# A product-key expert layer: 128 tokens' experts gathered row by row, 416 tokens through the dense product, u before v

## The reference, cut to what matters

```python
qh = (xt @ w_pq).reshape(PEER_BLOCK, PEER_HEADS, 2, half)
sub = einsum('thcd,ckd->thck', qh, sub_keys)
top_s, top_i = lax.top_k(sub, PEER_TOPK)
cand = (top_s[:, :, 0, :, None] + top_s[:, :, 1, None, :]).reshape(PEER_BLOCK, PEER_HEADS, 256)
best_s, best_c = lax.top_k(cand, PEER_TOPK)
...
experts = i1 * PEER_KEYS + i2
gate = jax.nn.softmax(best_s, axis=-1)
act = jax.nn.gelu(einsum('td,thkd->thk', xt, expert_u[experts]))
return einsum('thk,thkd->td', gate * act, expert_v[experts])
```

## Time and profile before

| | |
|---|---|
| median of three runs | 2608.47 us (2607.95 to 2617.67) |
| profiled execution | 2607.49 us |
| its span, first to last instruction | 2605.7 us |
| PE busy | 2344.5 us (90%), 12881 matmuls |
| DVE busy | 1535.3 us (59%) |
| POOL busy | 1064.4 us (41%) |
| ACT busy | 830.9 us (32%) |
| DMA | 411.09 MB |
| routing with 46 u blocks | about 914 to 1209 us |
| gate tables with 16 u blocks | about 1209 to 1507 us |
| value stage | about 1541 to 2594 us |

### The profile page before, as it was taken

The page is one execution under the profiler, slowest core; times in us unless marked ns, Lnnn a source line. Parts: engine busy times, 40 slices in busy tenths (PEclk is TensorE's granted clock), DMA queues, the critical chain, the costliest instruction groups (busy, mean ns, idle before and its releaser), DMA issues.

```text
span 2605.7 us, 36939 instructions
## 1 busy us (share of the span) xinstructions
PE 2344.5 (90%) x12881; PEld 1949.2 (75%) x12881; DVE 1535.3 (59%) x2958; ACT 830.9 (32%) x1293; POOL 1064.4 (41%) x568
## 2 busy tenths in 40 slices
PE   6999997775698999997777789999999999999998
PEld 5989557754488977776666668888888888888886
DVE  2567344333312089999999945555555555555555
ACT  3232332312223255553333332222222222222221
POOL 2334002310022244445777754444444445444442
PEclk9998579868998999998999999999999999999999
DMA  6441455428631143342433465555555555555553
GB/s 222 143 157 66 153 200 214 182 76 303 216 111 62 48 129 116 127 133 85 166 142 136 177 228 173 174 175 176 177 177 175 172 173 172 173 175 176 173 174 103
DMA packets 165036, 411.09 MB, mean 158 GB/s; under 512 B 11936, under 2 KB 82848, under 8 KB 159168
## 3 DMA queue, kind: packets, MB, share of 16 engines
q1 hardware_dynamic: 152672, 275.77, 32.6%
q10 hardware_dynamic: 3056, 100.53, 9.9%
q0 software_dynamic: 9216, 33.56, 3.4%
HBM read 351.95 MB, written 124.29 MB: 183 GB/s over the span
## 4 chain that ended last, share of the span: by engine, by line
PE 65%; issue 15%; POOL 10%; DVE 4%; DMA 3%; ACT 2%; SPq 1%; POOLq 0%; ACTq 0%; DVEq 0%; PEldq 0%
PE bank L2122 18%; PE bank L2124 18%; PE bank L2123 18%; POOL one L1497 6%; POOL u_lo L1591 3%; PE bank L427 1%; DMA ks<-kc 1%; PE bank L446 1%; PE bank L628 1%; SPq L937 1%; PE bank L618 1%; PE bank L627 1%; PE bank L436 1%; PE bank L2204 1%; PE bank L2195 1%
## 5 line engine op out<-in xcount | busy, mean ns | idle before, releaser
L1591 POOL TENSOR_TENSOR u_lo<-u_raw,u_hi 128x1024 fp32r<-128x1024 f32 x128 | 330.1, 2580 | 706.8 <-ACT u_hi L1573 706.8
L1716 DVE TENSOR_TENSOR y_t<-y_t,bank 128x512 f32<-128x512 f32 x512 | 351.9, 687 | 361.5 <-PE bank L2124 361.5
L2122 PE MATMUL bank<-hn_hi,u_hi 128*128 128x512 f32 x1024 | 409.0, 399 | 14.4 <-POOL u_lo L1591 13.7
L2124 PE MATMUL bank<-hn_hi,u_lo 128*128 128x512 f32 x1024 | 406.6, 397 | 0.0
L2122 PE MATMUL bank<-a_hi,v_hi 128*128 128x512 f32 x1024 | 400.1, 391 | 5.1 <-DVE a_lo L1711 5.1
L2123 PE MATMUL bank<-hn_lo,u_hi 128*128 128x512 f32 x1024 | 403.3, 394 | 0.0
L2123 PE MATMUL bank<-a_lo,v_hi 128*128 128x512 f32 x1024 | 399.6, 390 | 0.0
L2124 PE MATMUL bank<-a_hi,v_lo 128*128 128x512 f32 x1024 | 399.4, 390 | 0.0
L1772 POOL TENSOR_TENSOR v_lo<-v_raw,v_hi 128x1024 fp32r<-128x1024 f32 x128 | 304.8, 2405 | 8.7 <-ACT v_hi L1673 8.6
L2122 PEld LDWEIGHTS bank<-hn_hi,u_hi 128*128 128x128 f32 x1024 | 193.4, 189 | 65.0 <-POOL u_lo L1591 23.6
L2122 PEld LDWEIGHTS bank<-a_hi,v_hi 128*128 128x128 f32 x1024 | 192.6, 188 | 46.9 <-DVE a_lo L1711 5.2
(11 more groups left out here) (370 smaller groups left out, 4154.2 us busy)
## 6 DMA issues: line engine op xcount, KB each, us to landing
u_raw<-eu SPq DMA_DIRECT2D x128, 512.0 KB, 5.9
v_raw<-ev SPq DMA_DIRECT2D x128, 512.0 KB, 3.7
gates_dram<-gst ACTq DMA_DIRECT2D x8, 4096.0 KB, 12.2
gin<-gates_dram SPq DMA_DIRECT2D x64, 512.0 KB, 4.4
k_s<-kc ACTq DMA_DIRECT2D x29, 1104.0 KB
v_s<-vc ACTq DMA_DIRECT2D x29, 1104.0 KB
acts_dram<-act_c SPq DMA_DIRECT2D x64, 256.0 KB, 2.1
act_l<-acts_dram SPq DMA_DIRECT2D x64, 256.0 KB, 4.5
```

What stands on the lines that cost most here:

```text
L1591: nc.gpsimd.tensor_tensor(out=u_lo[s][:], in0=u_raw[s][:], in1=u_hi[s][:].bitcast(F32), op=ALU.subtract).then_inc(dn["ulo"], 1)
L1716: tt(out=y_t[:, x, :], in0=y_t[:, x, :], in1=bank[4 + x % 4][:], op=ALU.add).then_inc(dn["acc"], 1)
L2122: nc.tensor.matmul(out, ah, bh, start=first and i == 0, stop=False)
L2124: last = nc.tensor.matmul(out, al, bh, start=False, stop=final and i == n - 1)
```

## The change

128 of the 544 tokens (the last 96 of the prompt and the 32 sample tokens, `NG`) get their experts by index: they are routed first, each of their 128 picks is one indirect DMA that fetches one row of 1024 values for each of the 128 tokens, 128 fetches of u rows and then 128 of v rows, into three slots (`rows_g`). The other `DT` = 416 tokens go through the dense product. All 128 u blocks come first, in pairs with WINDOW = 6, 7, 7, 7, 6 beside the five routed tiles, two pairs beside each of eight gate blocks of 52 tokens, and 15 pairs behind them; then all 128 v blocks, with y accumulated in PSUM: its eight chunks stand in eight banks over all experts, and `accumulate` goes. All activations go through `acts_dram`, read for two experts at a time; gates are read for four.

The 128 dots stand on DVE between the steps of the routing (13 per tile from the second on), between the gate groups (46), and behind them (30). Of the 128 additions of v rows (`weigh`), 16 come before expert 2, the others at 112 of the places of experts 2 to 121. The fetches stand on POOL at matching places: those of u and the first 16 of v ahead of `lo_u` in each half of a pair, the others behind `lo_v` of an expert. One-hots are now made per token by tensor_scalar (compare with the pick, and in the second also multiply by the gate), and POOL's multiply goes. The core of the diff:

```diff
-GT = 64
-GBLOCKS = SEQ // GT
-SLOTS = P // (NB * NL)
-PICKS_S = PH * TOPK // SLOTS
+NG = 128
+DT = TOK - NG
+GBLOCKS = 8
+GT = DT // GBLOCKS
+PICKS = PH * TOPK
+ROUTE = [(DT, NG)] + [(t0, min(P, DT - t0)) for t0 in range(0, DT, P)]
+ROW_SLOTS = 3
...
-                        tt(out=one2[n % HOT][:], in0=bc(asc, 1, 4), in1=bc(cols_s[:, b % 2, 1, 4 * k:4 * k + 4], 2, PK), op=ALU.is_equal)
-                        tt(out=one1[n % HOT][:], in0=bc(asc, 1, 4), in1=bc(cols_s[:, b % 2, 0, 4 * k:4 * k + 4], 2, PK), op=ALU.is_equal)\
-                            .then_inc(ff["ones_raw"], 1)
+            for n in range(GBLOCKS * QUADS):
+                dve.wait_ge(ff["gate_mm"], n + 1)
+                for j in range(4):
+                    c = 4 * n + j
+                    ts(one2[n % HOT][:, j, :], asc, picks_t[:, 1, c:c + 1], None, ALU.is_equal)
+                    last = ts(one1[n % HOT][:, j, :], asc, picks_t[:, 0, c:c + 1], picks_t[:, 2, c:c + 1], ALU.is_equal, ALU.mult)
+                last.then_inc(ff["ones"], 1)
+                if n % QUADS % 2 and n >= HOT:
+                    dots(dve, NT, 1)
+            dots(dve, NT + 1, PICKS)
...
+            for x in range(XS):
                 for s in range(2):
-                    lo_u(pool, x + s, 1 - s)
-            pool_dense(pool, chain)
+                    for m in FETCH_X[2 * x + s]:
+                        fetch(pool, m)
+                    if s == 0 or x + 1 < XS:
+                        lo_u(pool, x + s, 1 - s)
+                if x in (FIRST_V, FIRST_V + 1):
+                    lo_v(pool, x - FIRST_V)
+            pool_dense(pool)
...
+        def fetch(pool, m):
+
+            if m == 0:
+                few_wait(pool, "idx", 1)
+            if ROW_SLOTS <= m < PICKS + ROW_SLOTS:
+                few_wait(pool, "dot", m - ROW_SLOTS + 1)
+            elif m >= PICKS + ROW_SLOTS:
+                few_wait(pool, "sum", m - ROW_SLOTS - PICKS + 1)
...
+        def dots(dve, stage, count):
+
+            for _ in range(min(count, DOTS[stage] - asked[stage])):
...
+                dve.wait_ge(row_in[n % ROW_SLOTS], 16 * (n // ROW_SLOTS) + 16)
+                row = rows_g[n % ROW_SLOTS][0:NG, :]
+                nc.vector.tensor_tensor_reduce(out=row, in0=row, in1=xrep[0:NG, :], scale=1.0, scalar=0.0, op0=ALU.mult, op1=ALU.add,
+                                               accum_out=pre_g[0:NG, n:n + 1]).then_inc(sx["dot"], 1)
...
+            def feed(i, q, last=False):
+
+                e = i * ROUND + q
+                if not last or q + 2 < ROUND:
+                    sp.wait_ge(dn["vlo"], e + 1)
+                    load_v(sp, e + 2, q % 2)
+                if q % 2 and (not last or q < 4):
+                    sp.wait_ge(dn["alo"], e + 1)
+                    load_acts(sp, i * (ROUND // 2) + (q // 2 + 2), q // 2 % 2)
+                if q % 4 == 3 and not last:
+                    sp.wait_ge(dn["mul"], e + 1)
+                    load_gates(sp, i * 2 + (q // 4 + 2), q // 4 % 2)
...
+            def outs(e, q, first=False, final=False):
+
+                pe.wait_ge(dn["alo"], e + 1)
+                pe.wait_ge(dn["vlo"], e + 1)
...
+        def act_value(act, f, q, arrived):
+
+            act.wait_ge(v_in[q % 2], arrived)
+            nc.scalar.activation(v_hi[q % 4][:], v_raw[q % 2][:], ACT.Copy).then_inc(dn["vhi"], 1)
+            act.wait_ge(dn["mul"], f + 1)
+            nc.scalar.activation(a_hi[q % 4][:], act_l[q // 2 % 2][:, q % 2, :], ACT.Copy).then_inc(dn["ahi"], 1)
...
+                f = i * ROUND + (q + 2)
+                act.wait_ge(dn["outs"], f + 1)
+                act_value(act, f, q + 2, i * (8 * ROUND) + (16 * ((q + 2) // 2) + 16))
...
+            for f in range(2, PK):
+                weight(f)
+                for m in FETCH_V[f - 2] if f - 2 < len(FETCH_V) else ():
+                    weigh(m - PICKS)
+                low(f)
...
+        def pool_dense(pool):
+            for f in range(2, PK):
+                lo_v(pool, f)
+                for m in FETCH_V[f - 2] if f - 2 < len(FETCH_V) else ():
+                    fetch(pool, m)
```

More of the change, by code:

```diff
@@ L1461, in dve_ffn @@
[L1461 to L1473 removed]
+            keep_picks(NT - 1)
@@ L1563, in pre @@
             for h in halves:
-                last = product(bank[s][:], [(u_hi[s][:, c, :], u_lo[s][:, c, :], hn_hi[:, c, 0:SEQ], hn_lo[:, c, 0:SEQ])
-                                            for c in range(h * CH // 2, (h + 1) * CH // 2)], first=h == 0, final=h == 1)
+                last = product(bank[s][:, 0:DT], [(u_hi[s][:, c, :], u_lo[s][:, c, :], hn_hi[:, c, 0:DT], hn_lo[:, c, 0:DT])
+                                                  for c in range(h * CH // 2, (h + 1) * CH // 2)], first=h == 0, final=h == 1)
             if 1 in halves:
@@ L1586, in gelu_ahead @@
                 act.wait_ge(act_out[s], 16 * x + 16)
-                gelu(act, x, s)
+                act.wait_ge(dn["pre"], 2 * x + (s + 3))
+                nc.scalar.activation(act_c[s][:], bank[s][:, 0:DT], ACT.Gelu).then_inc(dn["gelu"], 1)
         def lo_u(pool, x, s):
@@ new lines, in outs @@
+                    if first and out_bank(d) == 0:
+                        pe.wait_ge(dn["gelu"], 2 * XS + 2)
+                    last = product(bank[out_bank(d)][:, 0:DT], [(v_hi[q % 4][:, dc], v_lo[q % 4][:, dc], a_hi[q % 4][:], a_lo[q % 4][:])],
+                                   first=first, final=final)
+                    if final:
+                        last.then_inc(sx["ychunk"], 1)
+                if not final:
+                    last.then_inc(dn["outs"], 1)
+            pe.sem_inc(dn["outs"], 4)
@@ L1738, in dve_dense @@
-            dve.wait_ge(gate_out[1], 16 * (GBLOCKS // 2) + 16)
-            chain.link(nc.vector.memset(y_t[:], 0.0))
-            dve.sem_inc(dn["acc"], 4)
-            dve.sem_inc(dn["alo"], 4)
-            with dve.Fori(0, ITERS) as i:
-                for s in range(2):
-                    pair(i * 2 + s, s, i + AHEAD // 2, i)
-                    if s == 0:
-                        dot(i, gate_s[:, one(i)])
-                    else:
-                        weigh(i)
-                    accumulate(i * 2 + s)
@@ new lines, in dve_dense @@
+            few_wait(dve, "act", 1)
+            tt(out=coef[0:NG], in0=pre_g[0:NG], in1=gate_w[0:NG], op=ALU.mult).then_inc(sx["coef"], 1)
+            few_wait(dve, "coef", 1)
+            weight(0)
+            weight(1)
+            for n in range(EARLY_V):
+                weigh(n)
+                if n in (3, 7):
+                    low(n // 4)
+            for f in range(2, PK):
[3 more added lines that the diff above has]
+                low(f)
```

498 lines of the change are left out of this document (218 added, 280 removed).

## The result

The median went from 2610.84 us (four executions of the kernel before: the three whose median was on record and one more) to 2709.92 (2707.07 to 2710.91, four executions): a ratio of 1.037 with a 95% interval of 1.035 to 1.040, 99 us slower. The forecast was 2572, faster; it missed by 138 us.

The account below looks back on a forecast made before the run. It took DVE to bound the gate tables, PE the value stage (both full in routing). Routing to 1308, gate tables 313, other u blocks 164, value stage 774, end 11: span 2570, 2572 us with 1.8 around it; range 2445 to 2670.

Parts of the forecast that it names:

- 416 columns: PE matmuls: 0.187 us between starts by a straight line, so a block of 24 costs 4.5 us instead of 5.45.
- third rival: PE matmuls: 416 columns are no faster if a matmul cannot be shorter than 0.227 us; 2585 us, chance 0.04.
- Routing: Routing stage: DVE sets the end, 80.7 us per tile with dots at 1.8 each; ends at 1308, 99 us later.
- Gate tables: Gate-table stage: DVE bounds it at 39.5 us per block with u_lo blocking one-hots; 313 us, or 264 without the lock.
- the fetches on POOL stand ahead of u_lo; three row slots let them lead the dots: Routing stage: fetches are issued before their dots need them, their 0.95 us falling into POOL's waits.
- Other u blocks: 15 pairs behind the gate tables: PE needs 135 us, fetches make it 161, with the hand-over 164.
- slot rate of 2.77 us per fetch: Other u blocks: three slots, each free after landing 6.7, dot 1.3 and hand-overs 0.3, give one fetch per 2.77 us.
- Value stage: Last dense stage: 59 loop turns are 755 us; with shortened turns, filling and end, 774 us; PE alone 576.
- The loop: Value stage: low, weight, a_hi, v_hi, v_lo, fetch, landing, weigh, low; 6.8 us plus landing 6.0, 12.8 per two experts.
- Rows did not land early: Value stage rival: rows land in 4.2 us, loop 11.0; 2466 us, or 2417 without the tensor_scalar lock; chance 0.21.
- the slow rival: Value stage: rows land later than before under more traffic, 59 us per microsecond; 7.5 gives 2660 us; chance 0.22.
- The 3.2 estimated from the Trainium skill: Row fetches: an indirect load takes 2.0 us plus bytes at 436 GB/s, 3.2 for 512 KB; total 2407.

Follow-up runs that it names:

- run 9: run 8 with v_lo made on DVE, between weight and low, instead of on POOL; 2465.8 us.
- run 11: edits of run 6 and run 9 together, and DVE's wait for xrep moved to routing's second tile; 2405.38 us, 0.9225 of before.
- run 12: changed kernel without the last 112 fetches and weighs of v rows, so the output lacks these picks; 2476.3 us.
- Run 3: changed kernel with a fourth slot for fetched rows; 2706.2 us.
- run 4: changed kernel with no dots between the gate groups, the 46 moved behind them with the other 30; 2698.6 us.
- run 6: changed kernel with four row slots and every u fetch from the gate stage on half a pair earlier on POOL; 2654.1 us.
- run 13: changed kernel with only the routing's 52 u fetches and dots, the other 76 left out and counted as zero; 2566.5 us.
- Run 5: changed kernel with the value stage's first loads spread one by one behind the third to ninth pair of u blocks; 2708.5 us.
- run 8: changed kernel with v fetches two experts earlier, low ahead of weigh and four raw v buffers; 2526.51 us, 0.967 of before.

## Why the prediction was wrong, point by point

- **416 columns: right.** From 2209.80 to 2212.05 twelve steps between two matmul starts take 2.25 us, 0.187 each, as the straight line gave. The third rival is out: runs 9, 11 and 12 run the 128 experts in 579 to 580 us.

```profile
2209.80 0.35 PE L2135 MATMUL bank<-a_hi,v_lo 128*128 128x416 f32 x1
...
2212.05 0.35 PE L2135 MATMUL bank<-a_hi,v_lo 128*128 128x416 f32 x1
```

- **Routing: right but for small terms.** The tiles took 82.7 us ((1316.97 - 986.31) / 4) where 80.7 were forecast. DVE was not blocked as much as assumed (1.56 per dot with its read instead of 1.8), but waited 32 us for rows. The start was 5.5 us later than before; scores were ready at 918.16 and DVE began at 919.85, so the new wait for xrep cost 1.7 of it. The rest is older work, since the start lies between 910 and 922 in these runs.
- **Gate tables, 50 us: the step that failed is "the fetches on POOL stand ahead of u_lo; three row slots let them lead the dots", carried over from the routing.** Dots were charged with their work and no landing. A fetch stands ahead of the next u_lo but behind the last one, and that one waits, through ACT and PE, for DVE's own one-hots. It brought 61.7 us of waiting, of which the stage lost 50 against the forecast. Run 3 excludes the slots, run 4 shows the rest of the sum to hold, run 6 moves the fetch and lands at 311. That the rest holds so well is partly luck: in run 4 one-hots started every 0.196 and 0.256 us in turn, 0.226 in the mean instead of 0.21, and the 31 that u_lo caught cost some 69 us instead of 78.
- **Other u blocks, 31 us.** The slot rate of 2.77 us per fetch was not the bound: run 3's fourth slot gained nothing. Pairs with fetches took 11 us against 10.6 forecast, the last four 53 against 48. What the sum lacked are the bursts at its start. In run 13, without any fetch there, two pairs take 34 us where 18 would do, and in the change the first two pairs take 19 and 21.5. The fetches, which the forecast had charged, cost 19 in all (195 against 176). Run 5 shows that moving the first loads alone doesn't help. The gate store by itself was not tried, so which transfers make the burst stays open.
- **Value stage, 48 us: the mechanism was right, the terms too small.** The loop, its members, its two interleaved chains and 12.8 us came as forecast. From low of expert 3 (1897.37) to low of 121 (2663.47) it turned 59 times in 766 us, 13.0 each, for a forecast of 727. Four of the seven places without a pick lie in this chain; they shortened their turns to about 8, by 5 rather than 8 us: 20 us where the sum had 28. The other 55 turns took 13.4 in the mean, 31 us more than 12.8 makes. The term most mis-sized is weigh, 1.73 in the mean of all 128 instead of 1.28, because v_lo of the next expert blocked it; it gave 0.3 of the 0.6 in this chain, the landing of 6.2 instead of 6.0 another 0.2. In the chain of the even experts rows landed after 5.2, but v_hi waited for v loads that came late, and its turns were as long. The ends took 9 us more.
- **The rivals.** Rows did not land early (median 5.6 of all 256), and not late: the slow rival decides from 6.6. The sign flipped through waits in stages that no rival named. The forecast was 39 us under the time before, and the gate tables alone took more than that. A range of 2445 to 2670 for a sum with three new in-order loops, of which one had been costed, was too narrow upward.
- **The price of a row.** None of the 256 landed in less than 4.1 us (minimum, median, maximum below). The 3.2 estimated from the Trainium skill (DMA: Bandwidth & Descriptors, "Anatomy of one DMA — SWDGE (gpsimd) path") is not reached here; the measurement decides.

```profile
DMA to landing us min/median/max: 4.1/5.6/13.6
```

Not tried: the one-hots in their old form with POOL's multiply. Open: what makes a row take 5.6 us rather than 4.1.

## What to carry to other kernels

When a transfer's issue stands in one engine's queue behind work that waits, through the other engines, for the consumer of that same transfer, its whole landing enters the pace; look for that circle in every stage where the transfer occurs, not only in the one where you first saw it. The cure costs an index: issue it one or two rounds earlier (128 us here), and only then ask for more buffers. A fourth row slot alone gave 4 us, less than single executions differ by; two more v buffers behind the earlier fetch gave 50. When the loops are open, look for instructions that end just behind a POOL instruction beside them, and move one of the two.

## What the runs showed of the hardware

- A DVE instruction of the kinds below that begins beside a POOL subtraction waits for its end and then does nearly all of its own work: 0.27 became 2.46 (one-hot), 0.58 became 2.8 (weight), 1.28 up to 3.9 (weigh). The 25 caught one-hots of the change's gate tables (of 832, beside 31 u_lo) all ended 0.08 to 0.09 us behind u_lo, the 85 caught weights of run 8 from 1900 to 2350 ended 0.45 behind v_lo, and the 73 caught weighs of the change's value stage 1.08 or more. So it is not the instruction that is slow, and its length depends on when it began. This agrees with the Trainium skill (SBUF — State Buffer, "Who interferes with whom"): an exclusive lock, not a share. Unexpected was what it does to a loop: in run 8 it caught nearly every weight and so set the pace, and moving 1.23 us of work onto the busier engine, DVE, gave 54 us of the value stage.
- POOL's fetch instruction took 0.95 us in all 31 cases of the change's value stage in which no DVE instruction was running at its start, and 1.76 in the median of the 81 in which one was (weigh in 73 of them). It depends on which one: beside a dot, too, it took 1.76 (26 u fetches), beside a one-hot 0.95 (35), both in the median.
- DMA busy 0.93 of the time at 323 GB/s did not slow PE at all in run 9; landings of 6.1 us cost nothing there and set the pace in the change at 5.7.
